# Moving the scan's first wave under the projection of r in an RWKV stage

## The reference, cut to what matters

```
xs = x + mu0 * dx_prev + mu1 * dx_next                       # six mixes
r, k, v = xs[0] @ Wr, xs[1] @ Wk, xs[2] @ Wv
lw    = tanh(xs[3] @ w1[n]) @ w2[n]                          # w_lora
decay = exp(-exp(-softplus(-(w0[n] + lw)) - 0.5))
a     = sigmoid(a0[n] + (xs[4] @ a1[n]) @ a2[n])             # a_lora, the rates
g     = sigmoid(xs[5] @ g1) @ g2
kk    = k * k_k, divided by its norm over each head
kd    = k * (1 + (a - 1) * k_a)
S     = S * decay - (S kk) (kk * a)^T + v kd^T ;  y = S r    # along L, forward and backward
bonus = sum(r * (kd0 + kd1) * r_k) * v
out   = (norm(y0 + y1) + bonus) * g @ Wo
```

## Time and profile before

| | us |
|---|---|
| median of 3 runs | 2979.5 |
| the profiled execution | 2985.74 |
| its span | 2983.9 |
| TensorE busy in it | 2705.9 (91%) |
| VectorE busy | 2059.8 (69%) |
| ScalarE busy | 1546.1 (52%) |
| GpSimd busy | 75.8 (3%) |

### The profile page before, as it was taken

One profiled execution on the slowest core, in us unless ns is written; L12 is line 12 of the kernel. 1 busy time (PEld: TensorE's weight loads), 2 busy tenths in 40 slices (PEclk: granted clock), 3 DMA queues, 4 the chain that ended last, 5 costly groups with the idle time before them and its releaser, 6 DMA issues.

```text
span 2983.9 us, 50005 instructions
## 1 busy us (share of the span) xinstructions
PE 2705.9 (91%) x21328; PEld 2230.4 (75%) x21328; DVE 2059.8 (69%) x2958; ACT 1546.1 (52%) x2249; POOL 75.8 (3%) x93
## 2 busy tenths in 40 slices
PE   7779998879886899999999999996999989999988
PEld 7549996569874666666666666664997978988977
DVE  4656547374423598898989889897676865766864
ACT  3335432422111387777777777784446444446443
POOL 0000000020000000000000000000000011000011
PEclk9759999889995799999999999998999999999999
DMA  6104552200012198989989899993433544434532
GB/s 208 63 1 142 170 180 66 92 17 4 3 44 82 68 368 332 361 339 347 352 330 366 335 346 353 346 352 134 127 114 119 150 147 150 121 99 130 161 126 99
DMA packets 244416, 547.70 MB, mean 184 GB/s; under 512 B 24492, under 2 KB 187784, under 8 KB 200924
## 3 DMA queue, kind: packets, MB, share of 16 engines
q1 hardware_dynamic: 242204, 541.54, 51.4%
q0 software_dynamic: 1984, 2.89, 0.4%
HBM read 540.46 MB, written 1.05 MB: 181 GB/s over the span
## 4 chain that ended last, share of the span: by engine, by line
PE 76%; DVE 13%; ACT 6%; issue 2%; DMA 2%; SPq 0%; DVEq 0%; ACTq 0%
PE PS L158 19%; PE PS L160 19%; PE PS L159 19%; DVE wl L310 3%; ACT wh L301 3%; PE PS L349 2%; PE PS L1062 1%; PE PS L2326 1%; PE PS L570 1%; PE PS L1764 1%; DMA raw<-in_w_in 1%; PE PS L2290 1%; PE PS L1790 1%; PE PS L1090 1%; PE PS L2298 1%
## 5 line engine op out<-in xcount | busy, mean ns | idle before, releaser
L310 DVE TENSOR_TENSOR wl<-raw,wh 128x1024 fp32r<-128x1024 f32 (+2 forms) x630 | 744.6, 1187 | 422.1 <-ACT wh L301 402.6
L301 ACT ACTIVATE wh<-raw 128x1024 fp32r<-128x1024 f32 (+2 forms) x630 | 643.6, 1026 | 599.3 <-PE PS L160 526.2
L310 DVE TENSOR_TENSOR wl<-early,wh 128x1024 fp32r<-128x1024 f32 x384 | 465.8, 1222 | 54.4 <-ACT wh L301 34.6
L301 ACT ACTIVATE wh<-early 128x1024 fp32r<-128x1024 f32 x384 | 406.9, 1060 | 126.6 <-PE PS L160 117.8
L158 PE MATMUL PS<-b_hn_h,wh 128*128 128x256 f32 (+2 forms) x1312 | 376.3, 287 | 17.1 <-DVE wl L310 10.3
L160 PE MATMUL PS<-b_hn_h,wl 128*128 128x256 f32 (+2 forms) x1312 | 369.7, 282 | 0.0
L159 PE MATMUL PS<-b_hn_l,wh 128*128 128x256 f32 (+2 forms) x1312 | 369.1, 281 | 0.0
L158 PE MATMUL PS<-wh,xe_h 128*96 128x512 f32 x896 | 356.7, 398 | 1.2 <-DVE xe_l L1916 1.2
L159 PE MATMUL PS<-wl,xe_h 128*96 128x512 f32 x896 | 353.3, 394 | 0.0
L160 PE MATMUL PS<-wh,xe_l 128*96 128x512 f32 x896 | 353.1, 394 | 0.0
L158 PEld LDWEIGHTS PS<-b_hn_h,wh 128*128 128x128 f32 (+2 forms) x1312 | 230.7, 176 | 23.1 <-DVE wl L310 12.0
(11 more groups left out here) (473 smaller groups left out, 5198.5 us busy)
## 6 DMA issues: line engine op xcount, KB each, us to landing
early<-in_moe_in SPq DMA_DIRECT2D x128, 1024.0 KB, 4.9
raw<-in_moe_in SPq DMA_DIRECT2D x96, 1024.0 KB, 4.8
early<-in_moe_out SPq DMA_DIRECT2D x64, 1024.0 KB, 4.8
raw<-in_w_in SPq DMA_DIRECT2D x56, 1024.0 KB
raw<-in_moe_out SPq DMA_DIRECT2D x48, 1024.0 KB, 5.0
raw<-in_w_in SPq DMA_DIRECT2D x32, 704.0 KB
raw<-in_attn_w_in SPq DMA_DIRECT2D x12, 1024.0 KB, 5.5
raw<-in_rw_w_rkv SPq DMA_DIRECT2D x12, 1024.0 KB, 5.5
```

Source lines behind the costliest of these rows:

```text
L301: act.e.activation(st.two(n)[0], st.raw(n), ACT.Copy).then_inc(*act.sig("hi", st.name, n, sem=f"hi_{st.name}"))
L310: dve.e.tensor_tensor(lo, st.raw(n), hi.bitcast(F32), SUB).then_inc(*dve.sig("lo", st.name, n, sem=f"lo_{st.name}"))
```

## The change

1. The first wave's `first` (four groups) is issued by TensorE behind unit 3 of r, its `forward` behind unit 5; VectorE and ScalarE solve wave 0 before the last half of r is taken. `scan_order` no longer holds these steps for wave 0.
2. v's second half goes one unit at a time. Both `lora_out` stand ahead of k. k goes one unit at a time with the norm's sum two units behind; the squares use four buffers in place of eight.
3. VectorE multiplies the rates with the exponentials of the decays (BE = KA x a) before the norm is known, and BE with the normed kk later; the products with k are split in halves. ScalarE takes `exps(d)`, four squares and `k_part` of d in turn.
4. GpSimd's bonus waits for the last product of r instead of for `prep 1 ka`; two waits on it move in the scan.
5. Tiles are placed anew: mix 5 goes to the place of r, the squares behind the parts, and the tiles of wave 0 (`sc_n0`, `sc_pad`, `sc_lb`, `sc_xc`, `sc_tm`) behind the mix of r.

```diff
-        for u in (0, 4):
-            unsplit_units(pe, SA, "rv", range(u, u + 4), MIXED[2], T, ("mixed", 2))
+        unsplit_units(pe, SA, "rv", range(4), MIXED[2], T, ("mixed", 2))
+        for u in range(4, 8):
+            unsplit_units(pe, SA, "rv", [u], MIXED[2], T)
...
         lora_out("w_lora", rw_l)
-        for u in (0, 2):
-            unsplit_units(pe, SA, "k", range(u, u + 2), MIXED[1], T, ("mixed", 1))
         lora_out("a_lora", rw_l2)
...
+        for u in range(KC + 2):
+            if u == 2:
+                b, before = bank("k_norm")
+                pe.wait_ge(pe.at(*before))
+            if u < KC:
+                unsplit_units(pe, SA, "k", [u], MIXED[1], T, ("mixed", 1))
+            if u >= 2:
+                f = u - 2
+                pe.wait_ge(pe.at("k_sq", f))
+                e.matmul(PS[0:16, b, 0:T], by_head[:, f, :], rw_q[:, f % 4, :], start=f == 0, stop=f == KC - 1).then_inc(
+                    *pe.sig("k_norm_mm", f))
...
+        for u in range(8):
+            unsplit_units(pe, SA, "r", [u], MIXED[0], T, ("mixed", 0))
+            if u == 3:
+                for g in WAVES[0]:
+                    first(g)
+            if u == 5:
+                forward(0)
         scan_order(first, forward, lambda w, part: 0, back, level, pre, res, upd, out, grow)
...
         lora("w_lora", rw_c, "w0")
         lora("a_lora", rw_a, "a0")
+        for d in range(2):
+            exps(d)
+            for f in range(4 * d, 4 * d + 4):
+                k_square(f)
+            act.wait_ge(act.at("rate_taken", d))
+            for f in range(KC):
+                e.activation(rw_a[d][:, f, 0:T], ...).then_inc(*act.sig("k_part", d, f))
...
+        def half_k(d, f):
+            r = slice(f, f + 4)
+            dve.wait_ge(dve.at("k_part", d, f + 3))
+            dve.wait_ge(dve.at("k", f + 3))
+            e.tensor_tensor(rw_a[d][:, r], rw_a[d][:, r], rw_k[:, r], MUL).then_inc(*dve.sig("prep", d, "kd"))
+            dve.wait_ge(dve.last)
+            e.tensor_tensor(KA[d][:, r], KA[d][:, r], rw_a[d][:, r], MUL).then_inc(*dve.sig("prep", d, "ka"))
         decays(0)
         decays(1)
+        for d in range(2):
+            for f in range(4 * d, 4 * d + 4):
+                kk(f)
+            dve.wait_ge(dve.at("lora", "a_lora", 7, 1))
+            dve.wait_ge(dve.at("exp", d, "ka"))
+            e.tensor_tensor(BE[d], KA[d], rw_a[d], MUL).then_inc(*dve.sig("rate_taken", d))
+        for d in range(2):
+            half_k(d, 0)
+        dve.wait_ge(dve.at("k_norm_mm", KC - 1))
         e.tensor_scalar(n16, ps("k_norm", p=16), 1e-24, None, MAX).then_inc(*dve.sig("k_norm"))
         dve.wait_ge(dve.at("k_norm_root"))
         e.reciprocal(r16, n16).then_inc(*dve.sig("k_norm_r"))
         # the memsets, then for all f: rw_kk *= k_spread (both as before)
+        for d in range(2):
+            e.tensor_tensor(BE[d], BE[d], rw_kk, MUL).then_inc(*dve.sig("prep", d, "be"))
+            dve.wait_ge(dve.at("exp", d, "ke"))
+            e.tensor_tensor(KE[d], KE[d], rw_kk, MUL).then_inc(*dve.sig("prep", d, "ke"))
+        for d in range(2):
+            half_k(d, 4)
+        received(0, 4)                 # RE[d] *= rw_r, columns 0 to 3, both d
...
+        for g in WAVES[0]:
+            first(g)
+        forward(0)
+        for part in range(3):
+            solve(0, part)
+        received(4, 4)
         scan_order(first, forward, solve, none, level, pre, none, none, out, grow)
...
-        pool.wait_ge(pool.at("prep", 1, "ka"))
+        pool.wait_ge(pool.at("prep", 1, "re"))
```

More of the change, by code:

```diff
@@ L887, in levels @@
                         level(g, l, part)
-        for g in WAVES[0]:
-            first(g)
-        forward(0)
         for g in WAVES[1]:
             first(g)
[L893 to L896, removed]
+        for g in range(2):
+            pre(g)
         back(0)
@@ L1000, in rwkv_pe @@
             spread(b, f).then_inc(*pe.sig("k_spread_mm", f))
-        for u in range(8):
-            unsplit_units(pe, SA, "r", [u], MIXED[0], T, ("mixed", 0))
         def half(h):
@@ L1225, in k_square @@
             evacuated("k", rw_k, f)
-            e.activation(rw_q[:, f, :], rw_kk[:, f, 0:T], ACT.Square).then_inc(*act.sig("k_sq", f))
+            if f >= 4:
+                act.wait_ge(act.at("k_norm_mm", f - 4))
+            e.activation(rw_q[:, f % 4, :], rw_kk[:, f, 0:T], ACT.Square).then_inc(*act.sig("k_sq", f))
         lora("w_lora", rw_c, "w0")
[L1229 to L1232, removed]
         lora("a_lora", rw_a, "a0")
-        for f in range(4, 8):
-            k_square(f)
+        act.wait_ge(act.at("less_ka"))
+        for d in range(2):
[4 more added lines that the diff above has]
+            for f in range(KC):
+                e.activation(rw_a[d][:, f, 0:T], rw_a[d][:, f, 0:T], ACT.Identity, bias=less_ka[:, f:f + 1],
+                             scale=par("k_a", f)).then_inc(*act.sig("k_part", d, f))
         act.wait_ge(act.at("k_norm"))
@@ L1240, in rwkv_act @@
             e.activation(gh[0:w, j, :], ps("gate_h", j, p=w), ACT.Sigmoid).then_inc(*act.sig("gate_h", j))
[L1241 to L1248, removed]
+        for u in range(8):
+            evacuated("r", rw_r, u)
         def solve(w, part):
@@ L1276, in pre @@
                 act.wait_ge(act.at("scan_mm", nm, g))
+                if nm == "vt" and g == 1:
+                    act.wait_ge(act.at("bonus.kd"))
                 if nm == "vt" and g in (2, 3, 4):
@@ L1289, in upd @@
             e.activation(RU[g % 2], ps64("upd", g), ACT.Copy).then_inc(*act.sig("upd", g))
-        act.wait_ge(act.at("bonus.kd"))
         act.wait_ge(act.at("scan_zero"))
         none = lambda *x: 0
+        solve(0, 2)
         scan_order(none, none, solve, back, none, pre, res, upd, none, none)
@@ L1374, in rwkv_dve @@
         e.reciprocal(r16, n16).then_inc(*dve.sig("k_norm_r"))
[L1375 to L1393, removed]
         for x in (PAD, XC):
@@ L1403, in rwkv_dve, with received @@
         x.then_inc(*dve.sig("scan_zero"))
-        for f in (0, 4):
-            dve.wait_ge(dve.at("r", f + 3))
+        for f in range(KC):
+            dve.wait_ge(dve.at("k_spread_mm", f))
+            e.tensor_tensor(rw_kk[:, f, 0:T], rw_kk[:, f, 0:T], ps("k_spread", f), MUL).then_inc(*dve.sig("k_spread", f))
+        dve.wait_ge(dve.last)
+        for d in range(2):
[4 more added lines that the diff above has]
+            half_k(d, 4)
+        def received(f, n):
+            r = slice(f, f + n)
+            dve.wait_ge(dve.at("r", f + n - 1))
             for d in range(2):
-                e.tensor_tensor(RE[d][:, f:f + 4], RE[d][:, f:f + 4], rw_r[:, f:f + 4], MUL).then_inc(*dve.sig("prep", d, "re"))
+                dve.wait_ge(dve.at("exp", d, "re"))
+                e.tensor_tensor(RE[d][:, r], RE[d][:, r], rw_r[:, r], MUL).then_inc(*dve.sig("prep", d, "re"))
+        received(0, 4)
         def first(g):
```

31 lines of the change are left out of this document (12 added, 19 removed).

## The result

The changed kernel takes 2942.1 us (median of four runs, 2939.28 to 2943.91) beside 2978.7 for the kernel before (2974.71 to 2983.76): a ratio of 0.9875, with an interval of 0.9858 to 0.9893. The forecast was 2939.5, its range 2929 to 2959. The profiled execution took 2939.28 us with a span of 2937.4, which is 46.5 under the span before (2983.9); the medians differ by 36.6.

What follows compares the result with a forecast made beforehand. Bound: a chain of waits almost wholly through TensorE, with holes from transfers and handoffs. v 7.5, a_lora 2.2, lora and k 16.1, gate bank -3.2, slow r -2, wave 0 20.6, handoffs -1: gain 40, 2939.5 us, range 2929 to 2959.

Steps and rivals of the forecast that it cites:

- v (four units together, then four singly): v's second half: units 4 and 5 start without waiting for the fourth load; v ends at 502.0, gain 7.5 us.
- Both lora steps ahead of k: Loras and k: k's 5.69 us transfer and the slow clock behind it go; first k unit at 521.3, 525.38 before.
- VectorE sets the pace here: Decays and norm: scans from 518.5, new TensorE waits of 2.6 and 1.6 us, last norm sum at 559.2, 25.8 earlier.
- A wait the change adds: Second part of `gate_h`: TensorE waits 3.0 us for VectorE's norm read; r starts at 573.8, 22.6 earlier.
- r with wave 0 inside: r: `first` at 588.5, transposes 599.9, unit 6 waits 2.6 us, slow start 2 us; `pre` at 617.2 against 650.12.
- From there to `level`: From `pre` to `level`: the 6.3 us wait for pads goes, xl takes 3.5; `level` at 635.7, 41 us earlier.
- GpSimd at nothing: GpSimd's bonus, beside `first` of wave 1 and `pre`, adds nothing to VectorE's products there; other bound 13 us.
- Rival A: GpSimd slows VectorE in its new place, 13 us more on the path: gain 27, 2952.5 us; chance 0.07.
- The parts' shares inside the 20.6 us of wave 0: Wave 0 under r: 9.2 us of slowed products, memsets 3.1, full solve with handoffs, less 2.6 for the transposes' banks.
- D: Wave 0 doesn't run under r because operands are late; 18 of 41 us go: 2958; chance 0.13 together with B.
- B: VectorE stays late from 518 to 615, its chain slipping by one full exps: gain about 20, 2959; chance 0.13 with D.
- C: TensorE's clock stays low over k, r and gate_h because of new waits and thin products: +67, 3006; chance 0.03.

Runs made afterwards that it cites:

- the kernel of three edits: Kernel before with v's second half by single units, both loras ahead of k, GpSimd's bonus behind r's last product: 2948.5 us, 0.9890.
- the second profile: The changed kernel run once more with no edit: 2940.8 us, 0.9878 to the kernel before.

## Why the prediction was right, step by step

- *v (four units together, then four singly)*: 7.5 forecast, and 2.2 for a_lora's load, 9.7 together. The run with v by fours brings back both: 8.0 at the scans, 9.7 at r's start; alone in the kernel before, v brings 8.7. VectorE's mixes cap it at the 8.92 us that the scans had waited. Right, and the 2.18 us wait went.
- *Both lora steps ahead of k*: the end of the norm 25.6 us earlier, forecast 25.8 (559.4 and 559.2). The step names the 5.69 us transfer but not the larger wait that the order removes, 7.82 us for ScalarE ahead of the second lora's last products. It also leaves unsaid that the order of the loras does all of it beside v: with that edit alone the norm is 21.3 earlier, with both 28.8 (556.2 in the kernel of three edits).
- *VectorE sets the pace here*: scans at 518.2. Its two waits were smaller, 1.55 and 0.56 in place of 2.6 and 1.6: TensorE's third unit ended at 533.1 and not at 532.4, and `kk(0)` started 0.4 before its time. In the second profile the first wait was 2.90. The walk costed those waits but not the alternative, k in one block, which has none, nor the one in `gate_h`: r starts 5.9 us earlier with it.
- *A wait the change adds*: 2.58 us for 3.0, released by VectorE's read of the norm, as named. r at 573.5 for 573.8.
- *r with wave 0 inside*: `first` at 588.3 for 588.5, transposes at 599.97 for 599.9, unit 6 after 2.80 us for 2.6, `pre` at 617.2 to the tenth. The 2 us carried for a slow start of r were in fact 1.7 us in units 6 and 7 behind the wait of 2.80; in the second profile they were at r's start instead. The place was a guess, the size held. That `pre` came to the tenth is luck in part: in the second profile it is at 621.0.
- *From there to `level`*: the pads' wait goes, as forecast; late next is the evacuation of vt. The term that was mis-sized is `xl`: 5.20 us for 3.5, since the clock was at 0.68 there, behind two waits of 0.78 and 2.03 us with 1.7 us of work between. It was 4.94 before, at the same place behind the same 2.03, and that row was the one to take, though not a certain one: behind the same two waits it took 5.04 in the second profile and 3.52 with v by fours and with the bonus early. It is 1.7 of the 1.9 us by which `level` came late.
- *GpSimd at nothing*: right. 4.90 and 4.88 beside masks of 2.21 and 0.61. Rival A fell.
- *The parts' shares inside the 20.6 us of wave 0*: wrong in size. "9.2 us of slowed products" are worth 6.6 alone in the kernel before and nothing that can be told from zero in the changed one, and D's "18 of the 41 go" without overlap were 9 (`level`) to 12 (end of the scan). The total hid this: it came from the end times of a walk, and only the split into terms was wrong.
- *B and C*: no chain slipped by a full `exps`; the clock fell in single places (5.28 for one unit, 9.26 for two), never over a block of k or r.
- *Sum*: 40 forecast; 36.6 by the medians, 39.4 up to `level` in the profiles (36.1 in the second) and 46.5 over the span.

## What to carry to other kernels

Walk the new order engine by engine with measured durations: here it gave each end time within 2 us of one profile and 5 of another. But take the small instructions behind a handoff at the duration that they have there today, clock and all. Then undo each part singly and all together, and compare at the point where the change ends, for the untouched work behind it varied by 6 us. Here three short edits held most of the gain, a part that looked essential held none outside its own combination, and the later bonus was worth 6.6 us in one order and nothing measurable in the other. Before an interleave is kept, ask which waits it puts into the block that was dense.

## What the runs showed of the hardware

**VectorE and GpSimd take turns, a whole instruction each.** Beside GpSimd's product of 4.87 us, VectorE's product of two tiles in SBUF took 5.96 us in place of 1.29: it started at 628.36, 0.09 after GpSimd's, and ended at 634.32, 1.2 us (about its own time) behind GpSimd's end at 633.14. Timelines of the kernel before, VectorE's in the stretch 629 to 632 us:

```profile
628.36 5.96 DVE L1407 TENSOR_TENSOR rw<-rw,rw 128x1104 f32<-128x1104 f32 x1
```

And GpSimd's:

```profile
628.27 4.87 POOL L1532 TENSOR_TENSOR rw<-rw,rw 128x2208 f32<-128x2208 f32 x1 [627.82 <-ACT rw L1199]
633.23 5.78 POOL L1534 TENSOR_TENSOR rw<-rw,rw 128x2208 f32<-128x2208 f32 x1
```

GpSimd's next one, issued while VectorE's runs, is longer by 0.9, and so is the third (4.82, and 3.87 in the changed kernel), since VectorE's last stretched product reaches to 640.2. With the bonus early in the changed kernel it is 6.04 from the first on: both start at 617.61, and the lengths fit VectorE's being the first of the two. The Trainium skill ("SBUF — State Buffer", section Who interferes with whom) says that the order of issue decides who blocks, and tells of the full block for other forms of instruction; here plain products show it too. Products that read PSUM and one SBUF tile were not stretched: four of them took 2.20 or 2.21 us beside GpSimd's and without it.

**The clock falls in other places in two executions of one program.** The same kernel had one slow k unit and slow r units 0 to 3 in one profile, and slow units 6 and 7 in the other. It fell behind waits of 1.2 to 2.9 us here, shorter than the 4.64 us of the prediction's rival C, at r's start in the second profile with no wait at all but the thin spreads ahead of it (0.62 in 577 to 581 us), and not every time: behind the wait of 2.80 us in one profile (0.60), not behind the same wait of 2.79 us in the other (7.57 us for the two units behind it).
